# Experts' inputs scattered once into a table in pass order, instead of gathered pass by pass

## What is computed

```python
# 512 tokens (T), width 1024 (D), 32 experts, each token goes to its 4 best
top_val, top_idx = lax.top_k(logits, TOP_K)
gates = softmax(top_val)
...
hu  = xb @ w_up[e] + b_up[e]             # xb: the tokens of expert e; w_up[e]: 1024 x 2048
act = x_glu * sigmoid(1.702 * x_glu) * (x_lin + 1.0)
ys  = act @ w_down[e] + b_down[e]        # w_down[e]: 1024 x 1024
out = segment_sum(ys * gate, token)
```

## Time and profile before

| | |
|---|---|
| median of 3 runs | 2961.04 us (2953.68 to 2963.92) |
| the profiled execution's own time | 2956.22 us |
| its span | 2954.6 us |
| mean granted TensorE clock | 0.967 |
| busy: PE, DVE, ACT, POOL | 2770.8, 1125.3, 477.1, 242.1 us |
| read from and written to HBM | 626.43 and 24.06 MB |

### The profile page before, as it was taken

The page is one execution under the profiler, slowest core; times in us unless marked ns, Lnnn a source line. Parts: engine busy times, 40 slices in busy tenths (PEclk is TensorE's granted clock), DMA queues, the critical chain, the costliest instruction groups (busy, mean ns, idle before and its releaser), DMA issues.

```text
span 2954.6 us, 37476 instructions
## 1 busy us (share of the span) xinstructions
PE 2770.8 (94%) x15815; PEld 1366.1 (46%) x15815; DVE 1125.3 (38%) x1420; ACT 477.1 (16%) x936; POOL 242.1 (8%) x369
## 2 busy tenths in 40 slices
PE   7998989897889989898999999999999999999998
PEld 3445866332223323232333475467654334556763
DVE  3855454311111111111124253455436652444544
ACT  1113232000000000000001143000023662200001
POOL 1000011112111011110011500000000210000000
PEclk9988988999999999999999999999999999999999
DMA  9776235999999999999999131213132223321310
GB/s 340 286 257 255 74 115 191 385 345 416 384 394 408 409 404 408 407 413 397 413 407 350 9 127 52 86 57 114 57 80 59 66 50 114 107 86 57 114 57 29
DMA packets 172882, 648.23 MB, mean 219 GB/s; under 512 B 75965, under 2 KB 77573, under 8 KB 140305
## 3 DMA queue, kind: packets, MB, share of 16 engines
q1 hardware_dynamic: 156674, 607.76, 53.7%
q0 software_dynamic: 15984, 38.12, 4.1%
q10 hardware_dynamic: 64, 0.07, 0.0%
HBM read 626.43 MB, written 24.06 MB: 220 GB/s over the span
## 4 chain that ended last, share of the span: by engine, by line
PE 78%; DMA 12%; DVE 5%; ACT 2%; DVEq 1%; issue 1%; SPq 0%; ACTq 0%
PE ps L1867 14%; PE ps L2548 10%; PE ps L2583 10%; DMA slots<-in_w_down_dram 8%; PE ps L1905 8%; PE ps L2886 4%; PE ps L2619 4%; PE ps L2257 3%; PE ps L3142 2%; DMA slots<-in_ada_w_dram 2%; PE ps L1913 2%; PE ps L2513 2%; PE ps L2430 2%; PE ps L2533 2%; PE ps L1259 2%; DMA slots<-in_w_ada_dram 2%
## 5 line engine op out<-in xcount | busy, mean ns | idle before, releaser
L1867 PE MATMUL ps<-slots,hT 128*32 128x512 f32 x5120 | 563.2, 598 | 15.4 <-DMA slots<-in_w_up_dram 14.3
L1867 PEld LDWEIGHTS ps<-slots,hT 128*32 128x32 f32 x5120 | 165.5, 111 | 388.3 <-issue 362.6
L2583 PE MATMUL ps<-slots,work 128*128 128x512 f32 x672 | 289.6, 592 | 2.8 <-DVE work L2661 2.8
L1905 PE MATMUL ps<-slots,work 128*32 128x512 f32 x2112 | 247.8, 613 | 45.8 <-DMA slots<-in_w_down_dram 45.3
L2020 DVE TENSOR_SCALAR stage<-ps 128x512 f32<-128x512 f32 (+1 forms) x47 | 32.2, 686 | 549.0 <-PE ps L1871 548.6
L2583 PEld LDWEIGHTS ps<-slots,work 128*128 128x128 f32 x672 | 127.5, 190 | 162.5 <-issue 157.9
L2548 PE MATMUL ps<-hT,slots 128*128 128x256 f32 x768 | 168.7, 379 | 0.0
L1905 PEld LDWEIGHTS ps<-slots,work 128*32 128x32 f32 x2112 | 69.3, 112 | 194.5 <-issue 189.4
L2886 PE MATMUL ps<-hT,slots 128*128 128x512 f32 x352 | 156.8, 601 | 0.0
L2548 PEld LDWEIGHTS ps<-hT,slots 128*128 128x128 f32 x768 | 145.9, 190 | 22.4 <-issue 2.9
L2758 DVE TENSOR_TENSOR work<-work,ps 128x1024 f32<-128x1024 f32 x60 | 71.6, 1218 | 164.8 <-PE ps L2583 164.6
(11 more groups left out here) (610 smaller groups left out, 3447.7 us busy)
## 6 DMA issues: line engine op xcount, KB each, us to landing
slots<-in_w_up_dram SPq DMA_DIRECT2D x128, 2048.0 KB
slots<-in_w_down_dram SPq DMA_DIRECT2D x64, 2048.0 KB
slots<-in_mlp_w_dram SPq DMA_DIRECT2D x32, 2048.0 KB, 7.9
slots<-in_ada_w_dram SPq DMA_DIRECT2D x40, 1024.0 KB, 4.9
slots<-in_w_ada_dram SPq DMA_DIRECT2D x16, 1024.0 KB, 5.4
slots<-in_w_in_dram SPq DMA_DIRECT2D x5, 2048.0 KB
slots<-in_rnn_w_in_dram SPq DMA_DIRECT2D x24, 384.0 KB, 4.2
slots<-in_w_ada_dram SPq DMA_DIRECT2D x4, 2048.0 KB
```

Source lines behind the costliest of these rows:

```text
L1867: ins = pe.matmul(to, x[:, k, unit * UNIT:(unit + 1) * UNIT], upw[s][:, k % 2, col:col + CH], start=k == 0, stop=False)
L1905: ins = pe.matmul(to, actT[:, 4 * q + j, 64 * u + 32 * h:64 * u + 32 * h + 32], downw[sl[h]][:, j, half * CH:(half + 1) * CH], start=k == ...
L2583: ins = pe.matmul(ps[:, bank + t], x[:, k, t * P:(t + 1) * P], w[:, k], start=k == 0, stop=k == HK - 1)
```

## The change

- `h2` gets four buffers instead of two: `stage`, `tmp` and two in `scratch0` (in slots 2 and 3). DVE's and SP's waits for a free buffer are dropped.
- A table `xs_dram` of 3072 rows of 4 KB in HBM holds the rows in the order of the passes. `xs_fill` on POOL writes zeros over all of it (12.58 MB) in four transfers, before `route_fill`. The row of zeros also lies in slot 3.
- As soon as `slotf` is there, DVE casts it to `xslot` and a new step `ROUTE["slots"]` is signalled. POOL then issues 16 indirect scatters, four per tile of tokens: each writes the tile's 128 rows (524 KB) to the rows given by one choice. Pairs beyond an expert's capacity have an index out of bounds and are skipped.
- The gathers and `xsl` are gone, with the DVE and PE work for them. Instead SP loads a pass's rows from the table with plain transfers (`x_in`): 64, 96, or 128 and a rest, empty places included, 33 transfers and 2688 rows in all. They stand in SP's queue between the weights of w_up and w_down, two passes ahead.
- SP issues the first rows, and the first weights behind them, only when all 16 scatters and the four zero fills have landed (`xs_out`) and h2 is written. Rows for passes 1 and 2 wait for the steps `biases` and `listed`, those of pass 3 (and the w_down of pass 0 behind them) for `blocks`.
- `route_fill` clears one buffer of `work` instead of three pieces. `x_in` and `comb_in` share one semaphore, `tile_in`.

```diff
@@ buffers @@
+        h2_rows = [stage[:], tmp[:], scratch0[:, 10240:11264], scratch0[:, 13312:14336]]
+        zero_row = scratch0[:, 12288:13312]
...
+        XROWS = 24 * P
+        xs_dram = dram("xs_dram", (XROWS, D))
@@ mix_dve @@
-                dst = (stage, tmp)[t % 2]
-                if t >= 2:
-                    v.wait_ge(S("stage_free"), TURNED + PIECE["2"] + t - 1)
-                    v.wait_ge(S("h2_out"), 16 * (t - 1))
-                pairs_of = dst[:].rearrange("p (j r q) -> p j r q", r=2, q=P)
+                pairs_of = h2_rows[t].rearrange("p (j r q) -> p j r q", r=2, q=P)
@@ h2_sp @@
-                if t:
-                    sp.wait_ge(S("h2_out"), 16 * t)
-                sp.dma_start(h2_dram[t * P:(t + 1) * P], (stage, tmp)[t % 2][:]).then_inc(S("h2_out"), 16)
+                sp.dma_start(h2_dram[t * P:(t + 1) * P], h2_rows[t]).then_inc(S("h2_out"), 16)
@@ new, called after mod_turned_loads(g) @@
+        def xs_fill(g):
+            g.memset(zero_row, 0.0)
+            g.drain()
+            for q in range(4):
+                g.dma_start(xs_dram.rearrange("(p j) n -> p j n", p=P)[:, 6 * q:6 * q + 6], zero_row.unsqueeze(1).broadcast_to([P, 6, D])).then_inc(S("xs_out"), 16)
@@ route_fill @@
-            for at, n in ((0, D), (5120, 3 * D), (11264, D)):
-                g.memset(work[:, at:at + n], 0.0)
+            g.memset(xg[0], 0.0)
@@ route_pe @@
-                ins = pe.matmul(ps[0:64, 4, 0:2 * NQ], in_row[:, a], marks[:, a].rearrange("p two q -> p (two q)"), start=a == 0, stop=a == 15)
+                ins = pe.matmul(ps[0:64, 4, 0:NQ], in_row[:, a], marks[:, a, 1], start=a == 0, stop=a == 15)
@@ route_dve @@
             v.tensor_reduce(slotf, ohs, AX_X, ALU.add)
             v.drain()
+            v.tensor_copy(xslot[:], slotf).then_inc(S("route_step"), 1)
...
-            v.tensor_tensor(marks[:, :, 0], marks[:, :, 0], tok_of.unsqueeze(2).broadcast_to([P, 16, NQ]), ALU.mult)
...
-            v.tensor_scalar(xempty, ps[0:64, 4, NQ:2 * NQ], 0.0, float(T), ALU.is_equal, ALU.mult)
-            v.drain()
-            v.tensor_tensor(xsl[:], ps[0:64, 4, 0:NQ], xempty, ALU.add).then_inc(S("route_step"), 1)
@@ moe_sp @@
-            for i in range(NPASS + 1):
+            def x_in(i):
+                if i >= 4:
+                    sp.wait_ge(S("xg_free"), i - 3)
+                first = 2 * UNIT * QBASE[RANKS[i]]
+                for tile, r0, n, ks in x_runs(i):
+                    sp.dma_start(tile[0:n], xs_dram[first + r0:first + r0 + n]).then_inc(S(f"xg_in{i % 4}"), 16)
+
+            e = expert(0)
+            sp.wait_ge(S("xs_out"), 16 * (4 + TT * TOPK))
+            sp.wait_ge(S("h2_out"), 16 * TT)
+            x_in(0)
+            for j in range(4):
+                load(sp, up_slot[0][j], moe_up_w(e, j), up_rows[up_slot[0][j]])
+            sp.wait_ge(S("route_step"), ROUTE["biases"])
+            x_in(1)
+            sp.wait_ge(S("route_step"), ROUTE["listed"])
+            x_in(2)
+            for i in range(1, NPASS + 1):
                 if i < NPASS:
...
+                if i == 1:
+                    sp.wait_ge(S("route_step"), ROUTE["blocks"])
+                if i + 2 < NPASS:
+                    x_in(i + 2)
+                e = expert(i - 1)
+                for j, s in enumerate(down_slot[i - 1]):
+                    load(sp, s, moe_down_w(e, j), down_rows[s])
@@ moe_gather (removed) and moe_pool @@
-        def moe_gather(g, i):
-            if i >= 4:
-                g.wait_ge(S("xg_free"), i - 3)
-            settle(g)
-            for q, units, at in quads(i):
-                n = units * UNIT
-                to = xg[i % 4][q * 64:q * 64 + n] if q < 2 else xg_rest[0:n]
-                g.indirect_dma_start(to, None, h2_dram, bass.IndirectOffsetOnAxis(ap=xsl[0:n, at:at + 1], axis=0),
-                                     bounds_check=T - 1, oob_is_err=False).then_inc(S(f"xg_in{i % 4}"), 16)
...
+            g.wait_ge(S("route_step"), ROUTE["slots"])
+            g.wait_ge(S("xs_out"), 16 * 4)
+            settle(g)
+            for t in range(TT):
+                for j in range(TOPK):
+                    g.indirect_dma_start(xs_dram, bass.IndirectOffsetOnAxis(ap=xslot[:, TOPK * t + j:TOPK * t + j + 1], axis=0), h2_rows[t], None,
+                                         bounds_check=XROWS - 1, oob_is_err=False).then_inc(S("xs_out"), 16)
...
-                if i + 4 < NPASS:
-                    moe_gather(g, i + 4)
@@ turn_x (moe_pe) @@
-                came[i % 4] += 16 * len(quads(i))
+                came[i % 4] += 16 * len(x_runs(i))
```

More of the change, by code:

```diff
@@ L1394, in build @@
         tab = sb("tab", [1, E + 2 * MAXO + 1], I32)
-        xsl = sb("xsl", [64, NQ], I32)
+        xslot = sb("xslot", [P, 16], I32)
         ysl = sb("ysl", [P, NQ], I32)
@@ L1424, in build @@
         N_ROUTE = 9 * 16
-        ROUTE = {name: n + 1 for n, name in enumerate(("maxima", "mask", "ranks", "table", "marks", "rows", "turned", "outs", "biases", "listed", "edges", "first", "blocks"))}
+        ROUTE = {name: n + 1 for n, name in enumerate(("maxima", "mask", "ranks", "table", "slots", "marks", "turned", "outs", "biases", "listed", "edges", "first", "blocks"))}
+        def xs_fill(g):
[3 more added lines that the diff above has]
+                g.dma_start(xs_dram.rearrange("(p j) n -> p j n", p=P)[:, 6 * q:6 * q + 6], zero_row.unsqueeze(1).broadcast_to([P, 6, D])).then_inc(S("xs_out"), 16)
         def route_fill(g):
```

39 lines of the change are left out of this document (15 added, 24 removed).

## The result

| | before | changed |
|---|---|---|
| median | 2960.38 us | 3010.97 us |
| lowest and highest | 2953.68 to 2963.92 | 3006.09 to 3016.06 |
| profiled execution and its span | 2956.22, 2954.6 | 3006.09, 3004.4 |
| mean granted TensorE clock | 0.967 | 0.962 |
| written to HBM | 24.06 MB | 45.04 MB |

The ratio is 1.0174, with an interval of 1.0144 to 1.0203. Forecast were 2950 us and a range that ended at 2976.

The account below looks back on a forecast made before the run. PE bounds the experts up to 682 us, the weight stream to 1403 us, then PE again. Later start +17, gathers -36, plain rows +7 make -12, taken as -11: median 2950.0 us, range 2934 to 2976 us.

Parts of the forecast that it names:

- What bounds the kernel: Experts' stretch: PE rules up to 682 us, the weight stream to 1403 us, then PE; at most 70 us to save.
- When the weights start: Start of the experts: weights, now behind the scatters, are issued at 542.4 us, 31 us later than before.
- The step of 15 gaps of 1.27 us: POOL's 16 scatters: issued 1.27 us apart, the last 19.1 us after the first, at 533.7 us.
- rival 2: Scatters at the start: each carries a gather's 1.2 us, 19 us more; +8 us, 2969 us; chance 0.13.
- What of it reaches PE: First passes, to the third pass: of the 31 us later start, +17 us go into the middle zone.
- the seven gathers that were to be saved: Stream before the third pass: dropped gathers give back about 7 us net of the 31 us lateness.
- What the gathers cost: Middle zone: a gather costs 1.2 us beyond its bytes; dropping 37 saves 39 us, taken as 36.
- What plain rows cost: Plain row loads beside the weights: 0.3 us each taken, 7 us for 25; bounds nothing and 1.2 us each.
- rival 4: Start and middle: slower scatters and plain rows disturbing like gathers, together; about +30 us, 2991 us; chance 0.05.
- Rival 3: Middle zone: short rows amid long ones disturb, so plain rows cost 1.2 us each; +12 us, 2973 us; chance 0.12.
- Rival 1: Middle zone: PE binds sooner, half of the 36 us saving is lost; +2 us, 2963 us; chance 0.20.
- The marks named for a wrong prediction: New profile: weights start behind 550 us, rates dip beside plain rows, or PE's waits shrink by less than 30 us.

Follow-up runs that it names:

- the kernel of 2904 us: The kernel before, without the gathers from pass 4 on (those passes compute with old rows): 2904.25 us, ratio 0.9804.

## Why the prediction was wrong

**What bounds the kernel** held. Three zones, the stream in the middle one, nothing lost behind it. The waits for weights moved with the stream in every experiment (25 us without gathers in the kernel before, 42 with spread gathers, 87 in the changed kernel).

**When the weights start.** From the first store of h2 on, the first scatter came where it was forecast (521.51 less 7.35 is 514.2 us; forecast 514.6). The step of 15 gaps of 1.27 us failed: 29.0 us instead of 19.1, since DVE's split lay beside it. That was the mechanism that rival 2 named, at half of its size (10 us of the 19): the section of the Trainium skill cited there (DMA: Bandwidth & Descriptors, section SWDGE vs HWDGE vs iDMA) says that VectorE, in one of its faster modes, locks GpSimd out of the memory of the descriptors. The trace agrees that they get in each other's way, with issues of up to 4.23 us; which mode the steps ran in it doesn't show. The prediction played it down for one gather of 1.03 us at 524.16 us, but that row shows one issue beside one cast, and of another kind (96x992, bf16 to bf16, 1.18 us; 524.15 to 525.33 us). In the changed kernel too the scatter of 528.79 us, beside that cast, took 0.96; the long ones stood beside the steps on 32x3072 floats. The landing was over 4.5 us after the last issue, not 8.1, and this second miss hid a part of the first. Net, the weights started at 548.4 us on the forecast's clock, forecast 542.4.

**What of it reaches PE.** Forecast +17 us at the third pass, measured +27.5. The way of reckoning was sound (PE did give back part: of 36.5 us, 25.2 were left). Mis-sized were the later start, 6 us, and the seven gathers that were to be saved, 7 us: the plain rows in their place cost as much (together somewhat more than the 10.5 us missed). The stretches show it (columns as in the earlier trace rows):

```profile
555.00:570.00 15.00, 7.32 (x44) 2.57 (x48) 0.00 (x0) 1.87 (x2) 0.00 (x0) 0.55 0.92 368
570.00:585.00 15.00, 11.73 (x109) 3.34 (x101) 0.00 (x0) 0.00 (x0) 0.00 (x0) 1.00 1.01 381
```

The stream had 368 and 381 GB/s, not 427. PE, idle for 23.2 us, came back at a granted clock of 0.55 in the mean of the first stretch, so mostly at 1.2 GHz, and its first piece took 6.02 us; from 570 to 585 us it ran at 2.4 GHz, with 3.64 us a piece.

**What the gathers cost.** Forecast 1.2 us each beyond their bytes; the run without them gives 1.0. The size was nearly right, and the saving of 36 us some 7 too high. The reason was not: the prediction laid the cost to the gather as a kind of transfer, and spread over all partitions a gather loses most of it.

**What plain rows cost.** This is the step that failed most, with 39 of the 61 us between forecast and result. The term stood at 0.3 us each, without a row, with bounds of nothing and 1.2. Measured are 1.7 us: 28 transfers x 1.4 us more are 39 us (35 for the 25 that the forecast counted). With the 7 us above it makes 46 us, and the middle went from -29 to +17, where the profiles have +16.8. Two arguments carried the 0.3. The first, "they stand in the queue of the weights and need no second one", has the sign wrong: issued through ScalarE's queue they cost 27 us less. The second put the cost of a gather down to its kind. It didn't ask where its rows land: what the dips of the earlier trace rows have in common with the plain transfers, and what the results' scatters with their 128 half rows don't have, is landing on a part of the partitions. The rule of the 16 ports in the Trainium skill (SBUF — State Buffer, section Door 1: The DMA port swizzle) would have been a rival in its own right: rows on 64 partitions use the ports unevenly, whatever fetches them. The upper bound was no bound either, since a transfer in the weights' queue can cost more than the dearest row of before.

**The rivals.** In what they cost, rival 4 came true, 2 and 3 together, with a chance of 0.05. Its 2991 us were 20 short, since its price was that of a gather. Rival 3 had the effect, that plain rows disturb as much as gathers or more, but not the cause: it named short rows read amid long ones, and the same 4 KB rows cost 27 us less on every second partition, more of them 42 us less on all. The range ended at 2976 because this case was left out as unlikely; but 2 and 3 had evidence of their own each, and nothing made them exclude one another. Rival 1 didn't happen: PE had room, as the kernel of 2904 us shows. Its price was also added up wrongly (half of 36 us is 18, not 13), and the chances give faster 0.45, not 0.47.

**What cost nothing, as foreseen:** the zero fill (POOL issued it at 421 us and it was over by 455, 20 us later than forecast but ahead of the experts; the third pass of the kernel without scatters is only 2.4 us later than before), and SP's wait for `blocks` (13.4 us, until 587 us, while the pieces already queued kept the stream at 426 GB/s). The marks named for a wrong prediction appeared: dips beside the plain rows, waits that don't shrink, and weights behind 550 us (555.76; on the forecast's clock 548.4).

## What to carry to other kernels

Beside a saturated stream of loads, look first at which partitions a small transfer lands on. Here half rows spread over all 128 cost little more than their bytes, where whole rows on 64 or 96 partitions cost 1 to 3 us each on top. Try such transfers in another queue than the stream's; here that won 1.0 us each. Before a group of indirect transfers moves onto the path that others wait for, look at what VectorE does in those microseconds, and hold its large float steps back.

## What was unexpected about the hardware

- 64 rows of 4 KB take 1.6 to 2.0 us more from the stream on partitions 0 to 63 than on every second one; a 96-row transfer on partitions 0 to 95 takes 2.4 to 3.4 us more than one of 128 rows on all of them, beyond the bytes. Why 96 are worse than 64 stays open.
- Loading 128 rows where 64 or 96 are needed made the kernel 42 us faster.
- The DMA engines show it in bytes only: behind a narrow transfer their busy share stays 1.00 while the rate falls from 426 to 300 GB/s.
- One indirect scatter kept POOL up to 4.23 us beside DVE's float steps on 32 partitions; without them all but the first took 0.96 to 1.00 us.
- Of the narrow rows' 1.7 us per transfer about 1.0 us went when ScalarE's queue took them, and 0.7 us stayed. Why one queue makes them dearer isn't shown.
